# Memory attention: query units by pairs of heads, the first pair's lengths and scores inside the last query unit, all values ahead of the output's units

## The reference, cut to what matters

```python
x = x + memory_cross_attention(rms_norm(x, xattn_norm[l]), rms_norm(mem, xattn_mem_norm[l]), ...)

def memory_cross_attention(h, m, w_q, w_kv, q_gain, k_gain, w_o):
    q = rms_norm((h @ w_q).reshape(B, S, XATTN_HEADS, XATTN_HEAD_DIM), q_gain)
    kv = (m @ w_kv).reshape(B, M, 2, XATTN_HEADS, XATTN_HEAD_DIM)
    k = rms_norm(kv[:, :, 0], k_gain)
    v = kv[:, :, 1]
    s = jnp.einsum('bqhd,bkhd->bhqk', q, k).astype(jnp.float32) * (XATTN_HEAD_DIM ** -0.5)
    p = jax.nn.softmax(s, axis=-1).astype(v.dtype)
    o = jnp.einsum('bhqk,bkhd->bqhd', p, v).reshape(B, S, XATTN_WIDTH)
    return o @ w_o
```

## Time and profile before

| | us |
|---|---|
| median of 3 runs | 1938.47 (1936.24 to 1944.36) |
| profiled execution, its time | 1938.25 |
| profiled execution, its span | 1936.9 |
| TensorE busy | 1876.6 |
| VectorE busy | 1167.6 |
| ScalarE busy | 928.0 |
| GpSimd busy | 92.0 |
| the stage in layer 0, from the transposes of x's second half (458.95) to output unit 2 (489.47) | 30.5 |
| the same in layer 1 (1141.05 to 1170.30) | 29.25 |

### The profile page before, as it was taken

The page is one execution under the profiler, slowest core; times in us unless marked ns, Lnnn a source line. Parts: engine busy times, 40 slices in busy tenths (PEclk is TensorE's granted clock), DMA queues, the critical chain, the costliest instruction groups (busy, mean ns, idle before and its releaser), DMA issues.

```text
span 1936.9 us, 28290 instructions
## 1 busy us (share of the span) xinstructions
PE 1876.6 (97%) x11756; PEld 1576.1 (81%) x11756; DVE 1167.6 (60%) x1645; ACT 928.0 (48%) x1413; POOL 92.0 (5%) x59
## 2 busy tenths in 40 slices
PE   8999998999999999999989999999999999999999
PEld 6888887887888888888878888888878888878887
DVE  5555476665655565554666666555597548686556
ACT  5444563234544454445532345444445654555553
POOL 0000010040000000000100400000010000000000
PEclk9999998999999999999989999999999999999999
DMA  6755342023555557553420235655544456444454
GB/s 239 250 189 179 136 142 77 14 77 109 172 188 186 177 192 245 193 187 114 137 77 13 78 109 169 207 185 174 163 147 149 162 195 202 162 143 152 159 188 142
DMA packets 83616, 299.19 MB, mean 154 GB/s; under 512 B 9632, under 2 KB 10784, under 8 KB 83232
## 3 DMA queue, kind: packets, MB, share of 16 engines
q1 hardware_dynamic: 79328, 287.87, 44.7%
q10 hardware_dynamic: 3840, 8.03, 1.2%
q0 software_dynamic: 320, 1.48, 0.2%
HBM read 296.30 MB, written 1.05 MB: 154 GB/s over the span
## 4 chain that ended last, share of the span: by engine, by line
PE 91%; DVE 6%; ACT 1%; issue 1%; DMA 0%; POOL 0%; ACTq 0%; DVEq 0%
PE ps L340 23%; PE ps L342 23%; PE ps L341 23%; PE ps L365 2%; PE ps L367 2%; PE ps L366 2%; DVE wlo L322 1%; PE ps L806 1%; PE ps L1180 1%; PE ps L564 1%; PE ps L1564 1%; PE ps L1560 1%; PE ps L1183 1%; PE ps L1171 1%; PE ps L743 1%
## 5 line engine op out<-in xcount | busy, mean ns | idle before, releaser
L322 DVE TENSOR_TENSOR wlo<-raw,whi 128x1024 fp32r<-128x1024 f32 (+1 forms) x546 | 663.5, 1223 | 428.4 <-ACT whi L313 427.2
L313 ACT ACTIVATE whi<-raw 128x1024 fp32r<-128x1024 f32 (+1 forms) x546 | 572.7, 1053 | 536.4 <-PE ps L342 461.7
L340 PE MATMUL ps<-whi,a_hi 128*128 128x512 f32 x1696 | 678.3, 400 | 14.8 <-DVE wlo L322 8.9
L342 PE MATMUL ps<-whi,a_lo 128*128 128x512 f32 x1696 | 664.8, 392 | 0.0
L341 PE MATMUL ps<-wlo,a_hi 128*128 128x512 f32 x1696 | 663.9, 391 | 0.0
L340 PEld LDWEIGHTS ps<-whi,a_hi 128*128 128x128 f32 x1696 | 320.7, 189 | 87.3 <-issue 11.7
L342 PEld LDWEIGHTS ps<-whi,a_lo 128*128 128x128 f32 x1696 | 320.3, 189 | 69.0
L341 PEld LDWEIGHTS ps<-wlo,a_hi 128*128 128x128 f32 x1696 | 321.0, 189 | 62.9
L340 PE MATMUL ps<-whi,h_hi 128*128 128x512 f32 x320 | 124.9, 390 | 0.0
L342 PE MATMUL ps<-whi,h_lo 128*128 128x512 f32 x320 | 124.6, 389 | 0.0
L341 PE MATMUL ps<-wlo,h_hi 128*128 128x512 f32 x320 | 124.5, 389 | 0.0
(11 more groups left out here) (315 smaller groups left out, 1813.4 us busy)
## 6 DMA issues: line engine op xcount, KB each, us to landing
raw<-stream SPq DMA_DIRECT2D x546, 512.0 KB, 3.3
arena<-rows ACTq DMA_DIRECT2D x2, 1026.0 KB, 14.1
arena<-mem ACTq DMA_DIRECT2D x2, 1024.0 KB, 10.6
arena<-lora ACTq DMA_DIRECT2D x2, 768.0 KB, 7.0
arena<-rows ACTq DMA_DIRECT2D x2, 512.0 KB, 4.8
const_tables<-consts POOLq DMA_DIRECT2D x1, 901.0 KB, 4.8
arena<-band POOLq DMA_DIRECT2D x1, 544.0 KB, 4.0
x_res<-x SPq DMA_DIRECT2D x1, 512.0 KB, 3.6
```

The costliest lines, as they stand in the source:

```text
L313: self.split_hi.mark(act.activation(self.weights(self.whi, u), self.weights(self.raw, u), ACT.Copy), u)
L322: self.split_lo.mark(dve.tensor_tensor(self.weights(self.wlo, u), self.weights(self.raw, u), self.weights(self.whi, u).bitcast(F32), ALU.s ...
L340: pe.matmul(out, a_h, hi, start=start, stop=False, skip_group_check=True)
L342: last = pe.matmul(out, a_l, hi, start=False, stop=True, skip_group_check=True)
```

## The change

The query units are cut another way: a unit now holds 512 of the 1024 rows, and the 256 columns of one pair of heads. Unit 1 is rows 0 to 511 of pair 0, unit 2 the same rows of pair 1, unit 3 the other rows of pair 0, unit 4 of pair 1 (`pe_xq`). So pair 0 is complete after unit 3. All of x's tiles 4 to 7 are turned after unit 1. In the middle of unit 4 TensorE does the lengths of pair 0 and the score sets 0 and 1 (`pe_xa_first`). VectorE copies both pairs. After unit 4 follow score sets 2 and 3, the lengths of pair 1, and then probabilities and values set by set; all four sets of values come before output unit 1, where before two sets came after it.

```diff
     def pe_xa_scores(self, l, i):
-        pe.wait_ge(*(self.xa_act("q", l) if hp else self.xa_dve("q", l)))
+        pe.wait_ge(*self.xa_dve("q", l, hp))
...
+    def pe_xq(self, l, half, hp, between=None):
+
+        pe = self.nc.tensor
+        u, self.n_pe = self.n_pe, self.n_pe + 1
+        i = u % RING
+        pe.wait_ge(*self.split_lo(u))
+        pe.wait_ge(*self.turned_lo(("xa", l), 4 * half + 3))
+        for k in range(4):
+            if between is not None and k == 2:
+                between()
+            kt = 4 * half + k
+            for b in range(2):
+                cols, out = slice((k % 2) * S + b * P, (k % 2) * S + (b + 1) * P), self.half((0, 1), 2 * hp + b)
+                hi, lo = self.whi[i][:, k // 2, cols], self.wlo[i][:, k // 2, cols]
+                pe.matmul(out, hi, self.AHI[:, kt, :], start=kt == 0 and b == 0, stop=False, skip_group_check=True)
+                pe.matmul(out, hi, self.ALO[:, kt, :], start=False, stop=False, skip_group_check=True)
+                last = pe.matmul(out, lo, self.AHI[:, kt, :], start=False, stop=True, skip_group_check=True)
+        self.unit_used.mark(last, u)
+
+    def pe_xa_first(self, l):
+
+        self.pe_xa_length(l, 0)
+        self.pe_xa_scores(l, 0)
+        self.pe_xa_scores(l, 1)
+
     def pe_xa(self, l):
-        for n in range(4):
-            pe.wait_ge(*self.turned_lo(("xa", l), 2 * n + 1))
-            self.pe_unit_turned(n, [(self.half((0, 1), i), i * P, P, i % 2 == 0) for i in range(4)])
-            if n < 2:
-                self.pe_turn_x(("xa", l), self.TURN_BANKS["xa"], self.x_done(l, "mix", 1), 4 + 2 * n, 2)
-        self.pe_xa_scores(l, 0)
-        self.pe_xa_length(l, 0)
-        self.pe_xa_scores(l, 1)
+        self.pe_xq(l, 0, 0)
+        self.pe_turn_x(("xa", l), self.TURN_BANKS["xa"], self.x_done(l, "mix", 1), 4, 4)
+        self.pe_xq(l, 0, 1)
+        self.pe_xq(l, 1, 0)
+        self.pe_xq(l, 1, 1, between=lambda: self.pe_xa_first(l))
         self.pe_xa_scores(l, 2)
+        self.pe_xa_scores(l, 3)
         self.pe_xa_length(l, 1)
-        self.pe_xa_scores(l, 3)
         self.pe_xa_probs(l, 0)
+        self.pe_xa_values(l, 0)
         self.pe_xa_probs(l, 1)
-        self.pe_xa_values(l, 0)
         self.pe_xa_values(l, 1)
         self.pe_xa_probs(l, 2)
-        self.pe_xo(l, 0, 0)
         self.pe_xa_probs(l, 3)
         self.pe_xa_values(l, 2)
         self.pe_xa_values(l, 3)
+        self.pe_xo(l, 0, 0)
         self.pe_xo(l, 1, 0)
...
     def act_xa(self, l):
-        self.act_split(1)
-        self.act_turn_x(key, banks, gain, 4, 2)
-        self.act_split(1)
-        self.act_turn_x(key, banks, gain, 6, 2)
+        self.act_turn_x(key, banks, gain, 4, 4)
+        self.act_split(2)
         self.act_squares(key, self.X, [self.XN[:, t, :] for t in range(NT)])
         self.act_split(1)
-        act.wait_ge(*self.unit_used(self.unit(l, "xq") + 3))
-        m.mark(act.activation(two(self.xQT, 1), self.bank(1).rearrange("p (h k) -> p h k", h=2), ACT.Copy), "q", l)
-        act.wait_ge(*self.xa_dve("q", l))
-        for hp in range(2):
-            if hp:
-                act.wait_ge(*m("q", l))
-            m.mark(act.activation(two(self.xSQ, hp), two(self.xQT, hp), ACT.Square), "square", l, hp)
         for i in range(4):
+            if i < 2:
+                act.wait_ge(*self.xa_dve("q", l, i))
+                m.mark(act.activation(two(self.xSQ, i), two(self.xQT, i), ACT.Square), "square", l, i)
             self.act_xa_exp(l, i)
...
+    def dve_xa_q(self, l, hp):
+        dve = self.nc.vector
+        dve.wait_ge(*self.unit_used(self.unit(l, "xq") + 2 + hp))
+        self.xa_dve.mark(dve.tensor_copy(self.xQT[:, 2 * hp:2 * hp + 2, :],
+                                         self.bank(hp).rearrange("p (h k) -> p h k", h=2)), "q", l, hp)
...
     def dve_xa(self, l):
-        self.dve_split(1)
-        self.dve_turn_x(key, banks, gain, 4, 2)
-        self.dve_split(1)
-        self.dve_turn_x(key, banks, gain, 6, 2)
+        self.dve_turn_x(key, banks, gain, 4, 4)
+        self.dve_split(2)
...
         self.dve_split(1)
-        dve.wait_ge(*self.unit_used(self.unit(l, "xq") + 3))
-        m.mark(dve.tensor_copy(self.xQT[:, 0:2, :], self.bank(0).rearrange("p (h k) -> p h k", h=2)), "q", l)
+        self.dve_xa_q(l, 0)
         dve.wait_ge(*m("eps", l))
         self.dve_xa_length(l, 0)
         self.dve_xa_max(l, 0)
         self.dve_xa_max(l, 1)
+        self.dve_xa_q(l, 1)
+        self.dve_xa_probs(l, 0)
         self.dve_xa_length(l, 1)
         self.dve_xa_max(l, 2)
+        self.dve_xa_moved(l, 0)
+        self.dve_xa_probs(l, 1)
         self.dve_xa_max(l, 3)
-        self.dve_xa_probs(l, 0)
-        self.dve_xa_probs(l, 1)
-        self.dve_xa_moved(l, 0)
         self.dve_xa_moved(l, 1)
         self.dve_xa_probs(l, 2)
+        self.dve_xa_probs(l, 3)
         self.dve_xo(l, 0)
-        self.dve_xa_probs(l, 3)
         self.dve_split(2)
         self.dve_xo(l, 1)
```

More of the change, by code:

```diff
@@ L3263 @@
         seq += [ffn_units(n["ffn1_w_in"][l], n["ffn1_w_out"][l]), units(w), units(n["xattn_w_kv"][l]),
-                w_o[[0, 1, 4, 5, 2, 3, 6, 7]], units(n["xattn_w_q"][l]), units(n["xattn_w_out"][l])[[0, 2, 1, 3]],
+                w_o[[0, 1, 4, 5, 2, 3, 6, 7]], n["xattn_w_q"][l].reshape(2, 4, P, 2, S).transpose(0, 3, 2, 1, 4).reshape(4, P, 1024), units(n["xattn_w_out"][l])[[0, 2, 1, 3]],
                 ffn_units(n["ffn2_w_in"][l], n["ffn2_w_out"][l])]
```

## The result

The changed kernel takes 1944.26 us (median of 20 runs), the kernel before 1938.24 in the same comparison: a ratio of 1.0027, with a 95% interval of 1.0016 to 1.0038. That is some 5 us slower, within the 0.5% that was forecast as no change. The profiled execution has a span of 1943.2 us against 1936.9.

A forecast was written before the change was run, and what follows sets the result against it. TensorE, 91% of the chain, was taken to bound the kernel. The new order's -0.3 us at full clock plus 3.3 us of lost clock gave +3.0 on 1938.25, so 1941.3 us, range 1934 to 1948.

The forecast's parts named there:

- Step 1: Second half of x and the query units: turned tiles and last split are covered by 2.4 us; nothing is paid.
- Step 2: First pair inside query unit 4: VectorE's copy stands behind output unit 2's split; TensorE waits 1.65 us.
- Step 3: Second pair after query unit 4: TensorE waits 0.9 us for its copy; the old 2.28 us wait is gone.
- Step 4: Probabilities and values: VectorE's queue delays copies; waits of 1.9 and 0.9 us, then 0.3 for probabilities 3.
- Step 5: ScalarE's tail: the move for values 3 stands behind output unit 3's split; 0.5 us shows.
- The order at the full clock: Memory attention stage, both layers: with the full clock throughout, the new order is worth -0.3 us in all.
- The clock: Stage: one 1.2 GHz stretch of about 3.3 us per layer, costing 1.65 us each, 3.3 in both; bounds nothing to 9.5.
- the clock is kept: Rival for the stage: six waits, none over 2 us, lose no clock; -0.3 us, 1938.0 us; chance 0.20.
- the waits go as intended: Rival for the stage: 2.5 us of waits in place of 6.2, full clock; -7.7 us, 1930.5; chance 0.06.
- half clock throughout: Rival: TensorE stays slow from first stall to output units; +15.7 us, 1954; chance 0.12, shared with two long stretches.
- the chain carries the stage's loss to the end: Contradicts the no-net-effect rival, where ffn2's weight stream takes back the gain or loss: 1938.3 us, chance 0.07.
- a difference outside the two stages: Sign of being wrong: any difference outside the memory attention stages of the two layers.

The follow-up runs named there:

- e4: Kernel before with only the new cut of the query units, splits behind them; scores to output units in the old order: 0.9992 of before.
- e1: Changed kernel with VectorE's copy of the first pair's queries ahead of its split for output unit 2: 1942.59 us, 1.0016 of before.
- e3: Changed kernel with 29 unread matmuls more per layer in three waits of the stage: 1944.38 us, 1.0006 of before.
- e11: Kernel before with 7 unread matmuls per layer in the mixer, ahead of L806: 1933.06 us, 0.9960 of before.
- e2: Changed kernel with VectorE's copy of probabilities 0 ahead of the second lengths and maximum 2: 1.0049 of before.
- e5: Changed kernel's cut with another order of scores, lengths and VectorE's and ScalarE's queues behind it: 1934.28 us, 0.9963 of before.
- e12: Changed kernel with 7 unread matmuls per layer in the mixer, ahead of L806: 1937.69 us, 0.9986 of before.
- e9: e5 with 7 unread matmuls per layer in the mixer, ahead of L806: 1921.6 us, 0.9903 of before.
- e8: Kernel before with 18 unread matmuls per layer in its 2.28 us wait before the first probabilities: 1.0007 of before.
- e10: e9 with 18, 20 and 24 more unread matmuls per layer in the mixer, the 18 misplaced: 1916.68 us, 0.9885 of before.

## Why the prediction held, and where it was off

The forecast was 1941.3 us in a range of 1934 to 1948, no change within 0.5%; 1944.26 lies in the range, about 5 to 6 us over before where 3.0 was forecast. The direction and the causes were right, one term was half its size, and the agreement of the whole with the stages owed something to luck.

- Step 1, the cut is free: right (e4), and no engine waited for the last query unit's split.
- Step 2, the copy of the first pair behind the split of output unit 2: right in place and cause (e1 moved just that). VectorE, after, shows the split and the copy right behind it (start, duration):

```profile
474.38 1.23 DVE L322 TENSOR_TENSOR wlo<-raw,whi 128x1024 fp32r<-128x1024 f32 x1 [0.78 <-ACT whi L313]
475.52 0.68 DVE L1838 COPY arena<-ps 128x512 f32<-128x512 f32 x1
```

  The wait was 1.40 us where I had 1.65: I started it at the last matmul's issue, the profile at its end.
- Step 3: 0.79 for 0.9. Step 4: 1.80 for 1.9 and 0.78 for 0.9; the 0.3 us for probabilities 3 did not come, and not in e3 at the full clock either, so that estimate was wrong, and the clock is not the reason. Step 5: 0.27 for 0.5. In sum 5.0 for 6.2; about half of the difference is the offset of each wait's start, the rest the 0.3 us and the tail.
- The order at the full clock: 29.75 us per layer by my sum (488.7 - 458.95), 29.70 and 29.71 in e3, and against the old order as it ran, 59.41 - 59.77 = -0.36 us where I had -0.3. That term was right, though with waits 1.1 us too long in it: half of that is only where a wait is said to start, the rest was made up elsewhere, which is luck.
- The clock was the term that was mis-sized. I took one stretch of 3.3 us per layer, 1.65 us; there were two in each, after the first and the third wait, and they cost 3.0 us (e3). The price of the first was right: e1, which removed it, gained 1.65 us beyond the wait. The second, behind the 1.80 us, had no term in the sum, only in the bound. With 3.0 in place of 1.65 the forecast would have been 1944.0. Why the clock fell behind just these waits stays open: e1 and e3 show that without them it was kept, but e11 kept it behind 2.46 us and e2 lost it behind 0.88, 1.00 and 0.78 us, so their length alone does not decide.
- The rivals: "the clock is kept" fell with the windows; "the waits go as intended" fell with the 1.40 and 1.80 us, though e5 shows that the same cut can do it; half clock throughout did not come, some 6.8 us of 32.7 were at 0.50; the chain carries the stage's loss to the end, as far as the medians of e11 and e12 tell (4.6 us for 4.5 in the stages).
- Of the signs, the stage took 32.7 us where 29 to 32 was to be right, by the clock of the second stretch, and a difference outside the two stages, a sign of being wrong, was there: 8 us each way, which cancelled.
- A part that I had given no term: the kernel's own spread outside the stage, 8 us in a layer, larger than the effect of the change. It is clock as well: of the ten traces with an unfilled mixer six show the long stretch in layer 0 and seven in layer 1, of the four with e9's fill none. The times of all executions say the same. The 20 of the changed kernel run from 1938.77 us at a mean granted clock of 0.982 over 1944 at 0.979 to 1953.28 at 0.974. Whether the stretch falls on the changed kernels more often than on the kernel before stays open: both traces of the latter show it in layer 1 and neither in layer 0, and one trace for each of the others can't tell chance from cause.

The Trainium skill's sentence on the clock (TensorE: Matmul & The Clock Gate, "What's actually happening"), that activity releases the half speed, is borne out by e3, e8 and e9, where activity alone, useful or not, held it. That six small pieces of idling would keep it released, as I had drawn from it, is not: the clock fell behind the waits of 1.40 and 1.80 us.

## What to carry to other kernels

A step that is pulled forward to hide it must be pulled forward in every queue that it passes: here TensorE's order was changed and VectorE's copy was left behind a split that nobody needed yet. Filling the waits of a trace with matmuls that nobody reads is a cheap experiment that parts the price of a wait from the price of the clock that it loses. Where the wait can't be removed it can be a gain: e9 to e12 were faster as a whole for their fill, e3 and e8 only in their stages. Look in the trace whether the fill lies in the wait that it was meant for (in e10 one did not). And where the whole disagrees with the stage that was changed, look at the granted clock of the stages that were not.

## What was not expected of the hardware

- A wait of 1.40 us before one-column matmuls was followed by 3.4 us at 1.2 GHz, and 1.80 us alone by some 3.3 us; 0.78 us behind two-column matmuls was followed by 15 us at a mean clock of 0.54 in one execution and at 1.00 in another of the same instructions. A wait of 2.46 us kept the clock in e11 and lost it in e12.
- Such a stretch cost 0.44 us for each of its us in the stage (3.0 for 6.8), though the other engines bound part of it.
- 29 matmuls more per layer made the stage 3.0 us shorter; 14 more in the whole kernel made it 12.7 us shorter (e5 to e9).
